# A router product on rows scaled only by the modulation, with the root, the shift and the bias brought in behind it

## The reference, cut to what matters

```python
def rms_norm(x, g):
    y = xf * lax.rsqrt(jnp.mean(xf * xf, axis=-1, keepdims=True) + EPS)
    return (y * g.astype(jnp.float32)).astype(x.dtype)
def modulate(h, shift, scale):
    return h * (1.0 + scale) + shift

def hier_moe(h, w_group, b_group, w_expert, b_expert, w_up, w_down):
    p_group = softmax(xf @ w_group + b_group)      # 4 groups
    g_idx = argmax(p_group); g_w = p_group[rows, g_idx]
    e_logits = (xf @ w_expert + b_expert).reshape(N, N_GROUPS, EXP_PER_GROUP)[rows, g_idx]
    top_w, top_i = lax.top_k(softmax(e_logits), TOP_K)
    ...
    return grouped_expert_mlp(xf, eid, top_w, w_up, w_down)
```

## Time and profile before

| | us |
|---|---|
| median of three runs | 1401.29 |
| profiled execution, its own time | 1403.53 |
| its span | 1401.7 |
| PE busy | 1242.1 (89%) |
| DVE busy | 546.5 (39%) |
| POOL busy | 399.1 (28%) |
| ACT busy | 376.2 (27%) |
| layer 0, mixer's last sum to the first expert's matmul | 450.5 to 503.7 |
| layer 1, the same | 1063.0 to 1116.0 |

### The profile page before, as it was taken

How to read it: one execution, slowest core, us unless ns; L and a number is a source line. 1 busy time by engine, 2 the same in 40 slices (tenths; PEclk the granted TensorE clock), 3 DMA queues, 4 the chain that set the end, 5 groups by cost and what they waited for, 6 DMA issues and landing times.

```text
span 1401.7 us, 21170 instructions
## 1 busy us (share of the span) xinstructions
PE 1242.1 (89%) x6989; PEld 796.2 (57%) x6990; DVE 546.5 (39%) x1315; ACT 376.2 (27%) x763; POOL 399.1 (28%) x747
## 2 busy tenths in 40 slices
PE   6999998999898779998784899999998499999867
PEld 4666677565476445554443766665674355555436
DVE  3121424776512532222111449998223522222214
ACT  2210036656301311111110345664203111111110
POOL 0200100300000134453332159986001224444420
PEclk9999999979999679999997899999898699999998
DMA  9776653000053269999984911113721589999955
GB/s 381 262 255 235 260 200 120 23 41 1 0 238 133 95 261 410 423 423 423 424 345 173 270 60 36 56 60 114 291 106 60 191 337 408 366 423 424 423 238 219
DMA packets 99943, 322.65 MB, mean 230 GB/s; under 512 B 16181, under 2 KB 49947, under 8 KB 77347
## 3 DMA queue, kind: packets, MB, share of 16 engines
q1 hardware_dynamic: 79280, 288.25, 52.0%
q0 software_dynamic: 12464, 21.91, 4.4%
q10 hardware_dynamic: 8131, 11.57, 2.3%
HBM read 312.41 MB, written 27.08 MB: 242 GB/s over the span
## 4 chain that ended last, share of the span: by engine, by line
PE 64%; SPq 10%; DMA 9%; DVE 7%; issue 5%; ACT 3%; POOL 3%; ACTq 0%; POOLq 0%; DVEq 0%
PE PS L649 10%; PE PS L1141 10%; PE PS L1014 9%; PE PS L695 8%; SPq L535 5%; PE PS L1036 5%; DMA ring<-in_moe_w_up 4%; PE PS L1082 3%; SPq L538 3%; PE PS L618 3%; PE PS L878 3%; DMA ring<-in_ada_w 2%; PE PS L999 2%; DVE scratch L1614 2%; DMA arena<-in_moe_w_up 2%
## 5 line engine op out<-in xcount | busy, mean ns | idle before, releaser
L1614 DVE TENSOR_TENSOR arena<-arena,PS 128x128 f32<-128x128 f32 (+3 forms) x109 | 40.3, 387 | 290.6 <-ACT arena L1509 287.0
L1014 PE MATMUL PS<-arena 128*64 128x256 f32 x1152 | 134.1, 383 | 13.5 <-DMA arena<-in_moe_w_up 12.4
L1141 PE MATMUL PS<-arena,ring 128*128 128x320 f32 x512 | 142.4, 440 | 3.5 <-issue 2.2
L695 PE MATMUL PS<-ring,arena 128*128 128x256 f32 (+1 forms) x640 | 143.3, 378 | 1.7 <-ACT arena L1321 1.7
L649 PE MATMUL PS<-arena,ring 128*128 128x320 f32 x512 | 140.0, 437 | 5.3 <-DVE arena L1902 3.7
L2392 POOL TENSOR_TENSOR arena<-arena 128x655 f32<-128x655 f32 x91 | 129.7, 1425 | 45.4 <-ACT arena L1580 32.6
L1014 PE MATMUL PS<-ring,arena 128*64 128x256 f32 x1056 | 127.0, 392 | 17.0 <-DMA ring<-in_moe_w_up 15.3
L695 PEld LDWEIGHTS PS<-ring,arena 128*128 128x128 f32 x640 | 117.1, 194 | 28.6 <-issue 14.5
L1141 PEld LDWEIGHTS PS<-arena,ring 128*128 128x128 f32 x512 | 98.4, 193 | 47.4 <-issue 9.1
L649 PEld LDWEIGHTS PS<-arena,ring 128*128 128x128 f32 x512 | 98.3, 192 | 46.4 <-issue 6.9
L2157 DVE SCALAR_TENSOR_TENSOR PS<-arena,vecT,PS 128x655 f32<-128x655 f32 x124 | 112.2, 905 | 4.2
(11 more groups left out here) (340 smaller groups left out, 1620.0 us busy)
## 6 DMA issues: line engine op xcount, KB each, us to landing
ring<-in_moe_w_up SPq DMA_DIRECT2D x64, 1024.0 KB, 16.5
arena<-in_moe_w_up SPq DMA_DIRECT2D x64, 1024.0 KB, 16.6
ring<-in_ada_w SPq DMA_DIRECT2D x48, 1024.0 KB, 9.0
ring<-in_moe_w_down SPq DMA_DIRECT2D x32, 1024.0 KB, 16.4
arena<-in_moe_w_down SPq DMA_DIRECT2D x32, 1024.0 KB, 16.8
arena<-y_rows ACTq DMA_DIRECT2D x10, 1024.0 KB, 8.0
ring<-in_od_w_in SPq DMA_DIRECT2D x16, 512.0 KB, 6.5
ring<-in_ev_w_in SPq DMA_DIRECT2D x7, 1024.0 KB, 16.0
```

Source lines behind the costliest of these rows:

```text
L695: last = pe.matmul(z_bank(i)[:, 0:n], hT[:, k, t * P:t * P + P], w[:, k, 0:n], start=(k == 0), stop=(k == KD - 1))
L1014: last = pe.matmul(PS[i * BLK:(i + 1) * BLK, 0, 0:2 * P].rearrange("p (a n) -> p a n", a=2), xblk[:, k, :], w[:, k % 4, :, i * P:(i + 1) * P],
L1141: last = pe.matmul(PS[:, 2 * a + n, 0:SEG], w[:, k, a, :], hT[:, k, n * SEG:(n + 1) * SEG], start=(k == 0), stop=(k == KD - 1))
L1614: return dve.tensor_tensor(out, a, b, op)
```

## The change

1. The norm does not make `hT` any more. Beside each slab's squares, ACT scales `xT` by the modulated gain into a new buffer `xA` (two instructions per slab, sample and context columns).
2. PE multiplies `xA` with the router's weights (`raw_logits`). Slabs go in pairs: an even slab writes partitions 0 to 63, an odd one 64 to 127, with up to 64 columns of weights (36 are wanted). Three of the four pairs stand ahead of `norm_sum`, the last behind it. `C_SEL` adds the halves where `rs` is turned back (`select_logits`).
3. The spreading matmuls, the diagonals and the 16 multiplications of `normed` are gone, and so are `shift_scale` and `ctx_mod` in front of the experts. DVE takes the reciprocal of the root, multiplies the logits by it and adds `lbias`, the bias plus the shift times the router's weights. `lbias` is made earlier: in layer 0 in the stage of the heads (`router_bias(0, 7)` on PE, `router_shift(0, 7)` on DVE), in layer 1 in the layer norm.
4. Turned rows: ACT copies them out of PSUM times the root (10 in a row, its two exponentials behind them), then POOL adds the shift to each tile (5 instructions on 128x1024), and SP writes the tile. The shift as a full row comes by DMA: SP writes it element by element to `shift_rows` and reads it back to all partitions.
5. `xA` lies over slots 12 to 14, so the order of the triples changes, and two of the first six experts are loaded behind `h_rows` (`e == NPLACE - 2`).
6. The chain behind `both` is shorter: one matmul for the counts, no scan and no extra add for the blocks, both choices in one instruction, 15 small instructions merged into 3; four instructions on the weights of tokens move behind the addresses.

```diff
-PLACES = ((3, 4, 5), (9, 10, 11), (12, 13, 14), (6, 7, 8), (0, 1, 2), (15, 16, 17))
+PLACES = ((3, 4, 5), (9, 10, 11), (6, 7, 8), (0, 1, 2), (12, 13, 14), (15, 16, 17))
 # SP, load_experts
+                        for c in range(2):
+                            sp.dma_start(shift_rows[2 * l + c].rearrange("(k p) -> p k", p=P), modT[:, l, 24:24 + KD, c], ...)
+                    if e == 2:
+                        sp.wait_ge(ev("shift_dma"), 64 * l + 32)
+                        for c in range(2):
+                            sp.dma_start(shift[c], shift_rows[2 * l + c].partition_broadcast(P)).then_inc(ev("shift_dma"), 16)
-                    if e == NPLACE - 1:
+                    if e == NPLACE - 2:
                         for t in range(NT):
-                            sp.wait_ge(ev("htok_a"), 2 * NT * l + 2 * (t + 1))
+                            sp.wait_ge(ev("h_tok"), NT * l + t + 1)
 # PE
+            def router_bias(l, b):
+                for c in range(2):
+                    for k in range(KD):
+                        last = pe.matmul(PS[:, b, ROUTE * c:ROUTE * (c + 1)], bc(modT[:, l, 24 + k, c:c + 1], [P, P]), wr[:, k, :], ...)
+                last.then_inc(ev("shift_mm"), 1)
+            def raw_logits(l, m):
+                pe.wait_ge(ev("xa"), KD * l + 2 * m + 2)
+                for n in range(2):
+                    for k in range(2 * m, 2 * m + 2):
+                        c = min(BLK, ROUTE * (KD - k))
+                        i = (k % 2) * BLK
+                        last = pe.matmul(PS[i:i + c, 2 * n, 0:SEG], wr_flat[:, ROUTE * k:ROUTE * k + c],
+                                         xA[:, k, n * SEG:(n + 1) * SEG], start=(m == 0), stop=(m == KD // 2 - 1))
             (norm_sum)
-                pe.wait_ge(ev("diag"), DIAG[2 * l + 1] + 1)
-                pe.matmul(PS[:, 4, :], ones, rs[:, 0:SAMPLE], start=True, stop=True)
-                pe.matmul(PS[:, 6, 0:CONTEXT], ones, rs[:, SAMPLE:T], start=True, stop=True)
             (heads, u == 2)
+                        router_bias(0, 7)
             (heads, u == 3)
-                        pe.wait_ge(ev("mod_c"), MODC + 5)
+                        pe.wait_ge(ev("coef"), BIASED[0])
 # ACT
             (norm)
                     act.activation(sq_sum if k == 0 else sq_one[k % 2], xT[:, k, :], ACT.Square)
+                    act.activation(xA[:, k, 0:SAMPLE], xT[:, k, 0:SAMPLE], ACT.Copy, scale=modA[:, q, k, 0:1])
+                    act.activation(xA[:, k, SAMPLE:T], xT[:, k, SAMPLE:T], ACT.Copy, scale=modA[:, q, k, 1:2])
-                for k in range(KD):
-                    act.wait_ge(ev("hn"), HN[q] + 2 * k + 1)
-                    shift_scale(q, k)
             (moe)
+                    act.activation(htok[:, t, 512 * half:512 * half + 512], PS[:, (1, 3, 7, 0)[i % 4], :], ACT.Copy,
+                                   scale=ss[:, 0, t:t + 1]).then_inc(ev("htok_a"), 1)
 # DVE, moe
-                normed(q)
+                dve.reciprocal(ss[:, 0, 0:NT], ss[:, 1, 0:NT]).then_inc(ev("coef"), 1)
+                link(tt(lgt[:, :, :], PS[:, 6, 0:NT * ROUTE]..., bc(ss[:, 0, 0:NT].unsqueeze(2), ...), ALU.mult))
+                tt(lgt[:, ST, :], lgt[:, ST, :], lbias[:, 1, :], ALU.add)
+                link(tt(lgt[:, 0:ST, :], lgt[:, 0:ST, :], bc(lbias[:, 0:1, :], [P, ST, ROUTE]), ALU.add))
+                link(dve.tensor_reduce(cnt[:, 0, :], PS[:, 6, 0:NT * EXPERTS]..., AX.X, ALU.add))
 # POOL, moe
+                pool.wait_ge(ev("shift_dma"), 64 * (l + 1))
+                for t in range(NT):
+                    pool.wait_ge(ev("htok_a"), 2 * NT * l + 2 * (t + 1))
+                    pool.tensor_tensor(htok[:, t, :], htok[:, t, :], shift[0 if t < ST else 1], ALU.add) \
+                        .then_inc(ev("h_tok"), 1)
```

More of the change, by code:

```diff
@@ L68 @@
 C_HALF = C_VAL + 2 * NT
-C_W = C_HALF + 1
+C_SEL = C_HALF + 1
+PAIR = BLK + ROUTE
+C_W = C_SEL + ROUTE
 V_ADAB, V_COND, V_NMIX = 0, 96, 112
@@ L90 @@
 A_HTOK = A_SLOT + 6 * SLOT
+A_XA = A_SLOT + 3 * SLOT
+A_SHIFT = (A_HTOK + 5 * D, A_HTOK - D)
 A_U = 5120
@@ L627, in norm_sum @@
                 last.then_inc(ev("sumsq"), 1)
-                pe.wait_ge(ev("diag"), DIAG[2 * l + 1] + 1)
-                pe.matmul(PS[:, 4, :], ones, rs[:, 0:SAMPLE], start=True, stop=True)
-                pe.matmul(PS[:, 6, 0:CONTEXT], ones, rs[:, SAMPLE:T], start=True, stop=True) \
-                    .then_inc(ev("spread"), 1)
             def project_out(l, kind, src, tile):
@@ L973, in moe @@
                         pe.wait_ge(ev("htok_a"), 2 * NT * l + i - 3)
+                    elif i == 3:
+                        pe.wait_ge(ev("gating"), GATING * l + 1)
                     for j in range(4):
-                        last = pe.transpose(quad((1, 2, 3, 7)[i % 4])[:, j, :],
-                                            hT[:, 4 * half + j, t * P:t * P + P], ident)
+                        last = pe.transpose(quad((1, 3, 7, 0)[i % 4])[:, j, :], xA[:, 4 * half + j, cols(t)], ident)
                     last.then_inc(ev("htok_t"), 1)
-                    if i == 0:
-                        turn_logits()
-                    if i == 6:
-                        ranks()
+                    if i == 1:
+                        select_logits()
+                pe.wait_ge(ev("gating"), GATING * l + 5)
+                pe.matmul(PS[:, 6, 0:NT * EXPERTS], ones, both[:, :, :].rearrange("p t n -> p (t n)"), start=True, stop=True) \
+                    .then_inc(ev("routing"), 1)
+                place = PS[:, 5, 0:NT * EXPERTS].rearrange("p (t n) -> p t n", t=NT)
+                pe.matmul(place, tri, both[:, :, :], start=True, stop=False)
+                for j in range(NT - 1):
+                    n = NT - 1 - j
+                    last = pe.matmul(place[:, j + 1:, :], ones, bc(both[:, j:j + 1, :], [P, n, EXPERTS]),
+                                     start=False, stop=(j == NT - 2))
+                last.then_inc(ev("routing"), 1)
                 pe.wait_ge(ev("gating"), GATING * l + 6)
@@ L1290, in norm @@
                         .then_inc(ev("squared"), 1)
+                    act.activation(xA[:, k, 0:SAMPLE], xT[:, k, 0:SAMPLE], ACT.Copy, scale=modA[:, q, k, 0:1])
+                    act.activation(xA[:, k, SAMPLE:T], xT[:, k, SAMPLE:T], ACT.Copy, scale=modA[:, q, k, 1:2]) \
+                        .then_inc(ev("xa"), 1)
                 act.wait_ge(ev("sumsq"), (NT + 1) * l + 1)
                 act.activation(ss[:, 1, 0:NT], PS[:, 4, 0:NT], ACT.Sqrt, bias=eps, scale=1.0 / D).then_inc(ev("root"), 1)
-                act.wait_ge(ev("coef"), q + 1)
-                for k in range(KD):
-                    act.wait_ge(ev("hn"), HN[q] + 2 * k + 1)
-                    shift_scale(q, k)
             def norm_tiles():
@@ L1485, in moe @@
                 norm(l)
-                act.wait_ge(ev("gating"), GATING * l + 3)
-                act.activation(rt[:, 0, :, 0:GROUPS], rt[:, 0, :, 0:GROUPS], ACT.Exp).then_inc(ev("gate_exp"), 1)
+                act.wait_ge(ev("coef"), RSTD[l])
                 for i in range(2 * NT):
@@ L1860, in _ @@
                     if u == 2:
+                        dve.wait_ge(ev("late_in"), 16 * 13)
+                        router_shift(0, 7)
                         dve.wait_ge(ev("h_c"), 3)
@@ L2186, in _ @@
                     coef(3)
+                    router_shift(1, 3)
             add_out(1)
```

179 lines of the change are left out of this document (88 added, 91 removed).

## The result

The changed kernel takes 1395.27 us (median of 9 runs, 1390.60 to 1397.16), the kernel before 1404.50 beside it (1399.92 to 1406.63). The ratio is 0.9932, 95% interval 0.9918 to 0.9946: 9.2 us faster where 16.1 were forecast, and 1.3 us outside the range. The profiled execution took 1396.16 us, its span 1394.3.

A forecast was written before the change was run, and what follows sets the result against it. Weights were taken to bound the experts' loop, whose stream the first expert starts. Terms 12.9 + 11.2 - 1 - 3.3 - 3.7 = 16.1 us off 1403.53 gave 1387.4, as a median 1385.2; range 1368 to 1394.

The forecast's parts named there:

- the mechanism of the collision: Gating chain: DVE instructions with two SBUF inputs and POOL's additions exclude each other for a whole instruction; 9.1 us lost per layer.
- Norm and logits: Layer 0, last slab to first reduction: reduction at 457.8 instead of 473.80, 16.0 us gone.
- 32 of them on 256 columns take 3.67 us, so 0.115 each: Price of PE's logit matmuls: 0.14 us each on 320 columns, 1.7 us for the first 12.
- POOL's additions: Five shift additions per layer beside the gating, 2.1 us each, 457.3 to 468.3 in layer 0; `both` 9.1 us later.
- one or two of them get in between two additions; some 7 pass: Gating: of 18 two-input DVE instructions some 7 pass while POOL adds; the remaining 11 need about 4.2 us afterwards.
- second rival: One instruction per addition, slower additions, and gathers behind two experts' loads: 1393 us, chance 0.12.
- first rival: POOL gives way or its additions hide, so gating runs as if alone: 1370 us, within 1366 to 1375, chance 0.24.
- Counts: From `both` to the positions' cast: 3.5 us instead of 8.6, so 5.1 us gone.
- one matmul with its wait 0.55: Counts: PE's counting matmul with its wait takes 0.55 us, ahead of seven steps of 3.0 us together.
- Bias in the layer norm: Layer 1: 16 bias matmuls ahead of the spreading matmul at 0.23 us each cost 3.7 us, bounds 2 and 4.
- Bias in the heads: Layer 0 heads: 16 bias matmuls, 2.1 us; second turn waits for `router_shift` until 257.8; cost 3.3 us, bounds 1.5 and 4.
- Loads and gather: Two experts' loads wait for the rows' write, first gather flies beside them: 1 us charged in layer 0, bounds 0 and 3.

The follow-up runs named there:

- e1_noadd: Changed kernel with its five POOL shift additions per layer replaced by one-column products, so the expert rows lack the shift; 1376.44 us, ratio 0.9803.
- e6_counts: Kernel before with the change's sixth point alone (shorter counts chain, merged gating products, later token weights); 1397.84 us, ratio 0.9942.
- e3_nobias: Changed kernel with the shift-times-router-weights product cut from 16 matmuls to 2 per layer, bias incomplete; 1378.57 us, total not usable because routing changed.
- e7_pieces: Changed kernel with each 128x1024 POOL addition cut into four of 128x256; 1392.11 us, ratio 0.9902.
- e2_memset: Changed kernel with each POOL addition replaced by two constant writes over the same tile; 1386.85 us, ratio 0.9875, with layer 1's routing changed.
- e4_psum: Changed kernel with the gating's intermediate results in PSUM, POOL's additions kept; 1379.39 us, ratio 0.9842.
- e12_all: e9_cast plus the sixth expert's load held until the first gather lands, and six and ten constant matmuls around the place matmuls; 1364.94 us, ratio 0.9712.
- e9_cast: e4_psum plus the bias made on POOL with one matmul, and the positions' sums in PSUM so the cast reads PSUM; 1372.07 us, ratio 0.9762.
- e11_warm: e9_cast plus matmuls on constants in each layer, six before the place matmuls and eight after; 1369.21 us, ratio 0.9741.

## Why the prediction was wrong

The direction and the mechanism of the collision were the forecast ones. What failed is the size of terms of the sum. The logits and the layer norm's bias were priced by rows whose time was divided by the records, as if each were an instruction, while a matmul leaves two; the bias in the heads was priced by turns. The counts left out PE's slow clock and a wait. So the time before the addresses was put too low, and the added matmuls too cheap, and the measured time lies 1.3 us above the range.

- **Norm and logits, first reduction 7.3 us behind the slab.** Without the additions (e1_noadd) it stands 8.8 us behind it. The step "32 of them on 256 columns take 3.67 us, so 0.115 each" failed: x32 in the earlier trace rows are 16 matmuls. The 12 logit matmuls took 3.45 us instead of 1.7 and the last four 1.29 instead of 0.56, so they end 5.8 us behind the slab instead of 4.8, and the sums over partitions wait 0.3 us for them. The selection was taken as now; but five matmuls (1.20 us) stand there in place of five turns (0.50), and with its wait it takes 1.6 us instead of 0.6. DVE's product on the logits came 7.9 us behind the slab, not 6.5: 1.4 us a layer.
- **POOL's additions, 9.1 us a layer.** Nearly right: they delay `both` by 9.7. The step "one or two of them get in between two additions; some 7 pass" holds about: 6 pass. `both` ended 24.0 us after the slab, not 22.0, because the additions start 1.1 us later (7.9 us behind the slab, not 6.8, since the turns stand behind the logit matmuls), take 11.66 us instead of 11.0 (2.33 us each where 2.1 was taken), and leave 4.45 us of chain instead of 4.2. The length of an addition is the second rival's, which named 1393 us and got 0.12; its slower gathers did not come. The first rival is refuted: 1376 us is what the kernel takes without the additions, not with them.
- **Counts, 3.5 us.** 4.55 in this kernel and in e6_counts alike. The seven steps on DVE took the forecast 3.0 us; what failed is "one matmul with its wait 0.55", which took 1.06, and a wait of 0.46 us for the rank matmuls at 483.81 that the sum put at nothing. Both stand at a granted clock of 0.50 behind 12.6 us without work on PE; at 0.85, in e1_noadd, the same stretch takes 3.8 us. With the two terms above: addresses 9.9 and 8.1 us earlier, not 12.9 and 11.2.
- **Bias in the layer norm, 3.7 us.** 7.04. The row that it was priced by, x10 in 2.29 us, stands for five matmuls (one for each tile), not ten. Divided by five it gives 0.46 us and 7.3 for the sixteen. The bounds of 2 and 4 had the same mistake, so the range could not catch it. The granted clock was 0.50 there, in this kernel as before the change.
- **Bias in the heads, 3.3 us.** That the number came near is luck; neither of its parts held. The sixteen matmuls were priced by turns, 0.13 us each, which leave one record; e1_noadd, with the same code, has them at full clock:
```profile
250.55 3.76 PE L648 MATMUL PS<-wr,modT 128*128 128x36 f32 x32
```
  That is 0.24 each and 3.76 instead of 2.1. And the wait for `router_shift`, forecast for 257.8, did not come: the second turn, at 262.64, follows PE's own matmuls without a gap; the wait showed itself at 258.02 only in e3_nobias, where the bias matmuls were gone. To the first scores the stage grew by 5.5 us in the profiled execution (from 244.07 before and 245.34 after) and by 2.2 in e1_noadd. The difference goes with the clock that PE was granted between 240 and 260, 0.90 in the one and 1.00 in the other (before: 1.00):
```profile
240.00:260.00 20.00, 19.15 (x90) 14.26 (x89) 11.26 (x30) 9.54 (x30) 6.21 (x11) 0.90 0.01 5
```
```profile
240.00:260.00 20.00, 19.15 (x96) 13.12 (x95) 11.31 (x28) 10.70 (x29) 6.67 (x11) 1.00 0.02 5
```
  (The columns are the stretch, its length, busy time of PE, weight loads, DVE, ACT and POOL, granted clock, DMA share, GB/s; first the changed kernel, then e1_noadd.) Of the other kernels with these matmuls, e7_pieces has the dip and 5.5 us, e2_memset and e4_psum have 1.00 and 2.2 us. Why the clock falls in some executions is open.
- **Not in the sum: the first expert.** Its matmuls took 6.37 us instead of 5.03 in layer 0 and 6.61 instead of 6.06 in layer 1, at a granted clock of 0.57 and 0.55 where it had been 0.72 and 0.59. e12_all, which fills most of PE's wait ahead of it, has 3.67 us at 1.00. Why the clock is lower than before the change, although PE's last idle time is shorter (6.9 against 7.4 us in layer 0), was not separated.
- **Loads and gather, +1 us.** Came out better: in the changed kernel the loads go out 14 to 11 us before the gather, which lands in 3.9 us (4.3 before). In the faster versions the charge would have been too small: 2.5 to 3 us in e1_noadd and e4_psum.
- **Right:** the saving passes through the experts' loop (from first refill to PE's last wait for weights 225.9 us before, 225.8 after), the rows' write is not last (the gather is released by DVE), the table load hides beside the additions, and POOL waits for ACT's copies and not for the shift's DMAs.

In numbers for the profiled executions: 6.1 us too few saved in the two stretches (2.9 by the logits, 1.1 by the additions, 2.1 by the counts), 3.3 too few charged in the layer norm, 2.2 in the heads, 1.9 for the two first experts, against 3.0 us that gathers did better and 2.0 us gained behind layer 1's first refill (to the end 277.4 us, before 279.4), with no cause of this change that I can name: 8.5 of the 8.7 us by which the span (7.4 us shorter) missed the 16.1.

## What to carry to other kernels

Before work goes to POOL beside a chain of small DVE instructions, count those that have two inputs in SBUF, and charge each one a whole POOL instruction until POOL is done. Putting one operand of each in PSUM took the cost away while POOL kept its work. When a new instruction is priced by a row, divide the row's time by the instructions in the code, not by the records in the row, take a matmul's price from a matmul and not from a turn, and look at the clock that the row had. And when a chain gets shorter, look again at what was issued beside its end: the gather issued at 492.8 us lands in 3.9, the one issued at 479.4 (e4_psum), nearer to the loads, in 6.9.

## What the runs showed of the hardware

- One DVE instruction with two SBUF inputs, or one scalar operation or cast from SBUF to SBUF, waits for the end of a POOL addition in flight (2.08 and 2.20 us beside additions of 2.33, 0.42 to 0.65 beside 0.71; the cast 1.62, the scalar operation 1.40). With one input in PSUM they took 0.18 to 0.21. Beside POOL's constant writes of 0.96 us two-input instructions from SBUF took 0.18.
- In the rows shown here a matmul in fp32 leaves two records and a turn one (5 matmuls x10, 8 turns x8). Sixteen matmuls of 36 columns took 3.76 us at a granted clock of 1.00 and 7.04 at 0.50.
- Behind one expert's load, layer 0's first gather landed 6.7, 6.1, 5.0 and 4.3 us after its issue when it was issued 3.3, 4.1, 5.1 and 5.8 us after the load, that is 10.0 to 10.2 us after the load's issue each time. Behind the loads of two experts, the first of them issued 4 to 9 us earlier, it took 6.1 to 6.9; with both issued 14 to 11 us earlier, 3.9.
- PE's granted clock after a wait was 0.50 or rose late, and filling the wait with matmuls on constants changed that. Place matmuls of layer 0: 2.39 us at 0.50 behind 6.9 us of waiting (e9_cast), 1.38 at 1.00 behind 1.3 us (e11_warm). First expert: 6.56 us at 0.55 behind 10 us without work (e9_cast), 5.46 at 0.66 behind 3.6 us (e11_warm), 3.67 at 1.00 behind 2.4 us (e12_all). The last wait alone does not set it: in e6_counts the place matmuls took 2.39 us behind 2.0 us, with PE at 0.50 already before that wait.
